# A hybrid attention and expert layer: rotary angles computed at the fourth tile, the second tile's norm between the weight splits, latent evictions one tile ahead, four gate blocks loaded ahead of the branch outputs

## The reference

```python
h = rmsnorm(x, g_mix)
proj = h @ w_in
(gq, gk, gv, gr, gaf, gab, cq, ckv, kr, gates) = jnp.split(proj, offs, axis=-1)
...
q_b = (rmsnorm(cq, mla_q_norm) @ w_uq).reshape(B, S, MLA_HEADS, hq)
kv = (rmsnorm(ckv, mla_kv_norm) @ w_ukv).reshape(B, S, MLA_HEADS, MLA_NOPE + MLA_V)
q_b = jnp.concatenate([q_b[..., :MLA_NOPE], rope(q_b[..., MLA_NOPE:], positions)], axis=-1)
...
y_a = o_a.reshape(B, S, GLA_HEADS * GLA_DV) @ w_gla_out
y_b = o_b @ w_mla_out
g = jax.nn.sigmoid(gates)
merged = g[..., :D] * y_a + g[..., D:] * y_b
x = x + merged @ w_o
x = x + expert_choice_ffn(x, ...)
```

## Time and profile before

| | |
|---|---|
| median of 3 runs | 2031.99 us (2028.87 to 2033.1) |
| the profiled execution | 2026.28 us, with a span of 2024.5 us |
| PE busy | 1919.2 us, 95% of the span |
| DVE busy | 1279.6 us, 63% |
| ACT busy | 1000.3 us, 49% |
| POOL busy | 117.4 us, 6% |
| mean granted clock of PE | 0.983 |

### The profile page before, as it was taken

The page is one execution under the profiler, slowest core; times in us unless marked ns, Lnnn a source line. Parts: engine busy times, 40 slices in busy tenths (PEclk is TensorE's granted clock), DMA queues, the critical chain, the costliest instruction groups (busy, mean ns, idle before and its releaser), DMA issues.

```text
span 2024.5 us, 26320 instructions
## 1 busy us (share of the span) xinstructions
PE 1919.2 (95%) x9396; PEld 1616.0 (80%) x9396; DVE 1279.6 (63%) x1676; ACT 1000.3 (49%) x1620; POOL 117.4 (6%) x127
## 2 busy tenths in 40 slices
PE   6989999999999999999899999998399999999997
PEld 6978888888778888888788888886288888888886
DVE  5457777777865656565311322533988989898986
ACT  5455555555454334243311211322277878777775
POOL 1110000000000000000000000000001010101010
PEclk9999999999999999999999999999699999999999
DMA  5200000000311111121412311252799999999992
GB/s 168 74 17 12 22 17 22 22 23 6 109 53 43 53 42 53 31 63 44 133 42 73 114 42 53 71 210 95 282 362 391 401 392 400 391 401 390 402 394 75
DMA packets 139731, 303.12 MB, mean 150 GB/s; under 512 B 16256, under 2 KB 70912, under 8 KB 139648
## 3 DMA queue, kind: packets, MB, share of 16 engines
q1 hardware_dynamic: 135040, 285.20, 37.8%
q0 software_dynamic: 4608, 16.78, 3.2%
HBM read 272.58 MB, written 29.36 MB: 149 GB/s over the span
## 4 chain that ended last, share of the span: by engine, by line
PE 87%; DVE 7%; ACT 2%; DMA 1%; issue 1%; SPq 1%; POOL 1%; DVEq 0%; ACTq 0%; POOLq 0%
PE ps L822 23%; PE ps L823 23%; PE ps L824 23%; PE ps L811 6%; PE ps L896 5%; PE ps L1092 1%; PE ps L930 1%; PE ps L929 1%; PE ps L1104 1%; PE ps L1198 1%; DVE row_max L1528 1%; PE ps L1076 1%; DMA d_raw<-in_w_in 1%; DVE top_i L1865 1%; PE ps L1102 1%
## 5 line engine op out<-in xcount | busy, mean ns | idle before, releaser
L1314 DVE TENSOR_TENSOR w_lo<-w_raw,w_hi 128x1024 fp32r<-128x1024 f32 x384 | 442.5, 1217 | 53.9 <-ACT w_hi L2310 53.7
L2310 ACT ACTIVATE w_hi<-w_raw 128x1024 fp32r<-128x1024 f32 x384 | 370.8, 1052 | 4.8 <-DMA w_raw<-in_w_gate_e 4.5
L1314 DVE TENSOR_TENSOR d_lo<-d_raw,d_hi 128x1024 fp32r<-128x1024 f32 x58 | 71.0, 1224 | 306.0 <-ACT d_hi L2095 305.8
L822 PE MATMUL ps<-w_hi,xeT_hi 128*128 128x512 f32 x512 | 201.0, 393 | 1.9 <-DVE xeT_lo L1314 1.0
L2095 ACT ACTIVATE d_hi<-d_raw 128x1024 fp32r<-128x1024 f32 x58 | 61.5, 1060 | 281.9 <-PE ps L824 270.0
L824 PE MATMUL ps<-w_hi,xeT_lo 128*128 128x512 f32 x512 | 199.4, 389 | 0.0
L823 PE MATMUL ps<-w_lo,xeT_hi 128*128 128x512 f32 x512 | 199.3, 389 | 0.0
L822 PE MATMUL ps<-hT_parts,d_hi 128*128 128x512 f32 x384 | 151.8, 395 | 6.1 <-ACT sg L2234 5.3
L824 PE MATMUL ps<-hT_parts,d_lo 128*128 128x512 f32 x384 | 150.3, 391 | 0.0
L823 PE MATMUL ps<-hT_parts,d_hi 128*128 128x512 f32 x384 | 150.3, 391 | 0.0
L1528 DVE TENSOR_REDUCE row_max<-ps 128x1 f32<-128x1024 f32 x64 | 78.3, 1224 | 106.1 <-PE ps L930 105.4
(11 more groups left out here) (322 smaller groups left out, 4090.0 us busy)
## 6 DMA issues: line engine op xcount, KB each, us to landing
w_raw<-in_w_gate_e SPq DMA_DIRECT2D x128, 512.0 KB, 7.1
w_raw<-in_w_up_e SPq DMA_DIRECT2D x128, 512.0 KB, 7.1
w_raw<-in_w_down_e SPq DMA_DIRECT2D x128, 512.0 KB, 6.0
d_raw<-in_w_in SPq DMA_DIRECT2D x80, 256.0 KB, 3.0
xs<-in_x SPq DMA_DIRECT2D x8, 512.0 KB, 12.1
rows_T<-hT SPq DMA_DIRECT2D x2, 2048.0 KB, 6.9
mla_out_T<-obS SPq DMA_DIRECT2D x16, 256.0 KB, 2.1
carry<-rows_T SPq DMA_DIRECT2D x1, 4096.0 KB, 14.2
```

The lines of the kernel that those rows point to most:

```text
L822: pe.matmul(out_ap, a_hi, b_hi, start=start, stop=False)
L1314: return dve.tensor_tensor(dst, whole, high.bitcast(F32), ALU.subtract)
L2310: nc.scalar.activation(w_hi[:, n % RING, :], w_raw[:, n % RAW, :], ACT.Copy).then_inc(hi_ok, 1)
```

## The change

Five moves, and no arithmetic is added or removed.

1. The gains and angles (DVE, 18 instructions from L1390 to L1414) leave the place ahead of the tile loop and stand in the loop at t = 3, behind `x_scale(5)` and ahead of `lat_in(3)`. ACT no longer waits for `small_in` ahead of the loop, but at t = 5. The sines are taken at t = 4 instead of t = 1.
2. `x_mean(1)` and `x_scale(1)` on DVE go between the splits of weight rows 5 and 7, and `x_square(1)` on ACT goes between rows 5 and 6.
3. PE transposes tile 1 behind step 6 of tile 0 instead of step 2.
4. The evictions of the latent blocks 0 to 4 stand one tile earlier on DVE and ACT.
5. SP issues the loads of jobs 2 and 3 ahead of the load of `mT[0:6]`, and not behind it and behind that of `mT[6:8]`.

```diff
-            load_jobs(0, 0, 2)
+            load_jobs(0, 0, 4)
             sp.wait_ge(oa_out, 16 * (GH - 1))
             sp.wait_ge(o_ev, GH * NT)
             sp.dma_start(mT[:, 0:6, :], ...).then_inc(oa_back, 16)
-            load_jobs(0, 2, 3)
             store_oa(GH - 1)
             sp.wait_ge(oa_out, 16 * GH)
             sp.dma_start(mT[:, 6:8, :], ...).then_inc(oa_back, 16)
-            load_jobs(0, 3, JOBS)
+            load_jobs(0, 4, JOBS)
...
-                    if k == 2 and t + 1 < NT:
+                    if k == (2 if t else 6) and t + 1 < NT:
                         x_rows_T(t + 1)
...
-            for k in range(2, KD):
+            for k in range(2, 6):
                 w_lat_low(k)
             x_mean(1)
+            w_lat_low(6)
             x_scale(1)
-            dve.wait_ge(small_in, 16 * small_loads)
+            w_lat_low(7)
+            def gains_and_angles():
+                dve.wait_ge(small_in, 16 * small_loads)
...
             for t in range(NT):
                 if t + 1 < NT:
                     x_low(t + 1, 0)
                     x_low(t + 1, 1)
+                if t == NT - 1:
+                    latents_T_in(4)
                 if t:
                     lat_scale(t - 1)
                 if t + 2 < NT:
                     x_mean(t + 2)
                     x_scale(t + 2)
-                for c in {6: (0,), 7: (2, 4)}.get(t, ()):
-                    latents_T_in(c)
-                if t == NT - 1:
-                    latents_T_in(6)
+                if t == 3:
+                    gains_and_angles()
+                if t >= 5:
+                    latents_T_in((0, 2, 6)[t - 5])
                 lat_in(t)
...
-            for k in range(4, KD):
-                w_lat_high(k)
+            w_lat_high(4)
+            w_lat_high(5)
             x_square(1)
+            w_lat_high(6)
+            w_lat_high(7)
             act.wait_ge(consts, 4)
-            act.wait_ge(small_in, 16 * small_loads)
...
-                if t == 1:
+                if t == 4:
                     for j, tbl in enumerate((sin_t, cos_t)):
...
-                for c in {6: (1,), 7: (3, 5)}.get(t, ()):
-                    latents_T_in(c)
+                if t == 5:
+                    act.wait_ge(small_in, 16 * small_loads)
+                if t >= 5:
+                    latents_T_in(2 * t - 9)
                 lat_squares(t)
```

More of the change, by code:

```diff
@@ L1382, in _ @@
             x_low(0, 1)
-            for k in range(2, KD):
+            for k in range(2, 6):
                 w_lat_low(k)
             x_mean(1)
+            w_lat_low(6)
             x_scale(1)
-            dve.wait_ge(small_in, 16 * small_loads)
[L1389 to L1411, removed]
-                                                     op0=ALU.mult, op1=ALU.add))
-                st.link(dve.tensor_scalar(dst[:], dst[:], shift, 3.1415925, ALU.add, ALU.min))
-                dve.tensor_scalar(dst[:], dst[:], -3.1415925, None, ALU.max).then_inc(trig_arg, 1)
+            w_lat_low(7)
@@ new lines, in gains_and_angles @@
+            def gains_and_angles():
+                dve.wait_ge(small_in, 16 * small_loads)
+                scale = 1.0 / math.sqrt(HQ)
+                st.mark(dve.tensor_scalar(qhn_c[:], qhn_c[:], scale, None, ALU.mult))
+                st.mark(dve.tensor_scalar(qhr_b[:], qhr_b[:], scale, None, ALU.mult))
+                dve.wait_ge(consts, 3)
+                st.link(dve.tensor_copy(pos_f[:], pos_i[:]))
+                st.link(dve.tensor_tensor(ang[:], pos_f[:].unsqueeze(2).broadcast_to((P, NT, RH)),
+                                          freq[:].unsqueeze(1).broadcast_to((P, NT, RH)), ALU.mult))
+                two_pi = 2 * math.pi
+                part1 = 6.25
+                part2 = float(np.float32(round((two_pi - part1) * 2 ** 14) / 2 ** 14))
+                part3 = two_pi - part1 - part2
+                for j, shift in enumerate((0.0, 0.25)):
+                    st.mark(dve.tensor_scalar(turns_f[:, j], ang[:], 1 / two_pi, shift, ALU.mult, ALU.add))
+                st.wait()
+                st.link(dve.tensor_copy(turns_i[:], turns_f[:]))
+                st.link(dve.tensor_copy(turns_f[:], turns_i[:]))
+                for j, (dst, shift) in enumerate(((sin_t, 0.0), (cos_t, math.pi / 2))):
+                    st.link(dve.scalar_tensor_tensor(out=dst[:], in0=turns_f[:, j], scalar=-part1, in1=ang[:],
+                                                     op0=ALU.mult, op1=ALU.add))
+                    for part in (part2, part3):
+                        st.link(dve.scalar_tensor_tensor(out=dst[:], in0=turns_f[:, j], scalar=-part, in1=dst[:],
+                                                         op0=ALU.mult, op1=ALU.add))
+                    st.link(dve.tensor_scalar(dst[:], dst[:], shift, 3.1415925, ALU.add, ALU.min))
+                    dve.tensor_scalar(dst[:], dst[:], -3.1415925, None, ALU.max).then_inc(trig_arg, 1)
```

## The result

| | before | changed |
|---|---|---|
| median | 2030.52 us (2028.87 to 2033.1, 4 runs) | 2006.62 us (2005.97 to 2009.48, 4 runs) |
| profiled execution's span | 2024.5 us | 2004.2 us |
| mean granted clock of PE | 0.983 | 0.986 |

The ratio is 0.9884, with an interval of 0.9867 to 0.9901. The direction was right, and the profiled execution's span was 2004.2 where 2005 was forecast. The profiled spans differ by 20.3 us and the medians by 23.9; the forecast was 19.5.

The account below looks back on a forecast made before the run. PE has little idle time, so the gain lies where it waits or runs at low clock. The terms 10.3 - 1.9 + 4.0 + 7.05 = 19.45 us, about 19.5 off 2031.99, give 2012.5 us; range 2007 to 2019, 8 in 10.

Parts of the forecast that it names:

- The bottleneck and the removed waits: PE's waits in latent and merge stages, behind small loads and angles, evictions and job g2's weights, are what can be won.
- the evictions: Latent stage: evicting blocks 0 to 4 one tile earlier removes PE's waits of 3.1 and 0.9 us, 4.0 us gained.
- The start: Latent stage: tile 1's first matmul at 22.1 instead of 31.55, tile 2's at 31.9 instead of 42.22, 10.3 us gained.
- The angles: Tile loop: the 6.10 us of angles on DVE make PE wait 1.05 and 0.85 us, 1.9 us given back.
- The merge stage: Job g2 starts without a gap: 5.35 us of wait and 1.7 us of slow clock, 7.05 us gained.
- The slack of y0: Merge stage: `oT_lo` is ready some 7 us before job y0 wants it, so y0 does not wait.
- The clock: Slow clock costs 1.7 us behind each of the 6.01 and 5.35 us gaps; the 3.14 us gap cost little.
- The conversion to a median: The profiled execution lies 5.7 us below the median, so the median is 2031.99 - 19.5 = 2012.5 us.
- The rivals: Five: new stalls cost clock 8%, only latent stage gains 6%, only merge stage gains 4%, no change 3%, slower 2%.
- The first: Rival: three new stalls (0.85, 1.05, 0.85 us) cost 1.7 us of clock each, 5.1 us more, 2017.6 us; chance 8%.

Follow-up runs that it names:

- e11: Changed kernel with the angle instructions in three parts at t = 2, 3 and 4, sines at t = 5: 2007.68 us, ratio to before 0.9892.
- e3: Kernel before with only SP's new load order (jobs 2 and 3 ahead of `mT`): 2022.16 us, ratio 0.9965.
- e8: Changed kernel with the load of job 3 left behind both loads of `mT`: 2010.68 us, ratio to before 0.9898.
- e13: Kernel before with its four long PE waits filled by 70 added matmuls, no wait shortened: 2024.71 us against 2030.55, ratio 0.9972.
- e1: Kernel before, unchanged, timed against itself: 2030.92 us (12 runs), in a second series 2029.31 (20 runs), ratio 1.0004.
- e9: Kernel before with 13 added matmuls in the 3.1 us wait for `cqT`, the wait not shortened: 2029.75 us, ratio 0.9998.

## Why the prediction was right or wrong

**The bottleneck and the removed waits: right.** All four long waits went, and for the reasons given: the small loads and the angles ahead of tile 1, the evictions behind tile 6's copies, the weights of job g2 behind `mT[0:6]`.

**The start: right, 1.1 us late.** Tile 1's first matmul was forecast at 22.1 and came at 23.23. The clock rose to the upper level (2.4 GHz) at about 17.0 in this execution and at 14.7 in the profile of before, and until then a matmul of 416 columns took 0.55 us instead of 0.35. The handoffs themselves held: from the transposes to this matmul 2.0 us were forecast and 2.07 measured.

**The angles: right.** 1.5 us of new waits (1.00 and 0.51), 1.9 forecast; e11 shows that they go when the angles are dealt out over three tiles.

**The merge stage: right.** 7.05 us forecast, 6.9 in the two profiles (20.3 less 13.4), 7.1 by e3's ratio (4.5 to 9.7). The table load took 1.28 us and the sigmoid began 0.01 us behind it, so the trace goes against the drain that ScalarE: Activation LUTs of the Trainium skill (What ACT_TABLE_LOAD costs) adds. The slack of y0 was right too: 7 us forecast, 8.0 measured (965.83 to 973.80). e8 cut it to 1.3 us, and PE did not wait for `oT_lo` even then.

**The clock: mis-sized, and this is the step that failed.** The prediction said of the 3.14 us gap ahead of tile 1's transposes that it "cost little", and priced the evictions at the 4.0 us of their waits, because the one profile showed the full clock behind both. Of six profiles with the gap ahead of the transposes, four have a slow stretch behind it: the mean clock over 19.4 to 25.4 us is 1.00 in two and 0.72 to 0.73 in four. Of five profiles with the 3.1 us wait for `cqT` unfilled, four have a slow stretch behind it: the mean clock over 90 to 104 us is 1.00, 0.76, 0.88, 0.88 and 0.88. The price of 1.7 us for the gap ahead of g2 was low as well: over the 12 us from g2's first matmul the mean clock is 0.88 in two of seven profiles and 0.74 to 0.78 in five. The sum held 3.4 us for clock in all, 1.7 each for the two longest gaps, and nothing for the other two; e13 puts the four gaps at 5.7 us (3.9 to 7.5). For the waits alone that leaves 16 to 18 us (the ratio 0.9972 of e13 less the two of the changed kernel, 0.9893 and 0.9884, times 2030), where the sum had 16.

**The conversion to a median: wrong for the same reason.** The step "2031.99 - 19.5" took the distance of 5.7 us between profile and median as given for both kernels. It was itself slow clock, most of it behind the gaps: the first profiled execution of before (mean clock 0.983) was one with few slow stretches, and the one of e1 (0.979) took 6.8 us longer. With the gaps closed, profile and median of the changed kernel lie 0.65 us apart. The distance was evidence of what the gaps cost, and was carried over as a constant. The 2031.99 us, a median of 3 runs, were also 1.5 us above that of the 4 runs of the result. That the span came out within 1 us of the forecast is in part luck: the other pairs of profiles (2024.5 or 2031.3 before, 2004.2 or 2006.0 after) differ by 18.5 to 27.1 us.

**The rivals.** None happened. The first looked at clock in the wrong place, at new stalls of 1 us: behind these the clock stays at 1.00. TensorE: Matmul & The Clock Gate of the Trainium skill (HAM oscillation) warns of loops that wait between bursts and start every burst at the lower clock. The traces agree for all 13 gaps of over 4 us, for 4 of 5 waits for `cqT` (3.1 us), and for none of the new stalls.

What stays open: what decides, behind the same wait, whether the clock falls; how much closing the waits of 2.0 to 2.7 us in the attention would give, where nothing was tried; and whether the fill of a single gap gains anything, which e9 could not tell.

## What to carry to other kernels

A gap on TensorE costs its length and, in many executions, clock behind it: here behind all 13 gaps of over 4 us, behind most of those of 2 to 3 us, and behind none that was shorter. One profile shows one draw of that. When a kernel's runs spread over several us and its profile sits at the fast end, read the spread as slow stretches behind the gaps and price a closed gap above its length. When a block of work must go into a loop, deal it out over several turns: one part of 6.1 us cost 1.5 us of new waits here, three parts of about 2 us cost none.

## What was not expected of the hardware

The same wait of 3.1 us for `cqT` was followed by the full clock in one execution and by a mean of 0.76 over 14 us in another. Waits of 2.5 us, in the attention, were followed by a slow stretch in 14 of 15 profiles. Adding 70 useless matmuls in idle time made the kernel 5.7 us faster and its executions almost three times as close together (3.0 against 8.6 us).
